# The order of six accumulating matmuls: by stationary tile, or by PSUM bank

## The chip, the cores and the metric

One Trainium2 chip; the kernel runs on one of its cores. The metric is the device time of the program in microseconds (us); smaller is better. The time before is 1608.74 us, the median of 3 runs.

## The reference

The program is one inference step of a small two-layer decoder, on 512 prompt tokens and 8 x 8 sample tokens, all in float32 (model width 1024):

```
x = x + rms_norm(mixer(rms_norm(x)))        # layer 0: chunked gated MLP, layer 1: RG-LRU block
x = x + rms_norm(swiglu(rms_norm(x)))
gmlp:   u, v = split(gelu(h @ w_in + b_in)); v = layer_norm(v); out = (u * (w_s @ v + b_s)) @ w_out
rglru:  y, xb = split(h @ w_in); conv of 4 taps; two gates by 8 blocks of 128x128; scan; out @ w_out
swiglu: g, u = split(h @ w_in); out = (silu(g) * u) @ w_out          # inner width 2816
```

Nearly all of the arithmetic is in the large products `h @ w`. Outputs are the two token results, the convolution and scan states, and the normalised `v` rows of the sample.

## The kernel before, in words

The 576 tokens lie on the free axis of all activations, which are stored transposed: feature tile by feature tile, 128 partitions x 576 columns. A product therefore has a 128x128 tile of the weights as its stationary operand and the activations as its moving operand. A PSUM bank takes 512 float32 columns, so an output tile of 576 tokens is a pair of banks, `2m` and `2m+1`, with 288 tokens (a "token half", `HT` = 288) in each. Four such pairs (`m` = 0 to 3) fill PSUM.

Every float32 product is done as three products of the reduced type `float32r`: the activation is split into a high part `hh` and a remainder `hl`, the weight into `whi` and `wlo`, and the result is `hh*whi + hl*whi + hh*wlo`. ScalarE makes the high parts (line 800 for weights), VectorE the remainders (line 1109). SyncE's queue loads weights into four slots of `stage` ahead of need.

A K step (`k`) of an output pair is thus six matmuls, three terms for each token half. The helper `three` (line 457) issues them. It is called by `u_body` (line 604), by the first and larger part of `out_phase` (line 644) and by `tile_unit` (line 722), in which one unit is one output pair over all 8 K steps. Its relative `one_half` (line 467) issues the three terms for one token half alone, all to one bank. It serves at the two kinds of stage border: in `first_tiles` (line 667), the first four output pairs of a projection, while the normalised activations are still arriving; and in the last four K steps of each group of `out_phase` (line 655), where half 0 is finished before half 1.

The order of the stages, with the start of the first matmul of 288 columns at 180 us: `V` (384-column matmuls with another helper, up to 180 us); `U`; then `out_phase("GO")`, `ffn_in("FI0")`, `out_phase("FO0")`, the `RI` projection with the recurrent block, `out_phase("RO")`, `ffn_in("FI1")`, `out_phase("FO1")`. Each `out_phase` has two groups (`G` = 0, 1) of four output pairs. In a group the K step is the outer loop and the pair `m` the inner one; in `tile_unit` the pair is fixed and K runs.

TensorE's instructions run in the order in which they are written. What other engines wait for are semaphores that the last matmul of a unit increments (`unit_done`, `y_tile_done`, `h_pair_used`); TensorE itself waits for weights (`lo_ready`), activations (`a_lo`, `h_lo`) and for a pair to be free (`pair_free[m]`, one semaphore for both banks of a pair). All of these waits stand ahead of a K step or a unit, none of them inside the six matmuls of `three`.

Of the kernel before, what the change touches and what calls it, by code (L numbers as in the profile page):

```python
# [38 lines left out]
def trunk_kernel(nc, x_prompt, x_sample, state_conv, state_h, norm_gains,  # L39
# [8 lines left out]
    HT = TT // 2  # L48
# [26 lines left out]
    with ExitStack() as ctx:  # L75
        def sb(name, shape, dt=F32):
            return ctx.enter_context(nc.sbuf_tensor(name, shape, dt))
# [6 lines left out]
        hh = sb("hh", [P, KD, TT], F32R)  # L84
        hl = sb("hl", [P, KD, TT], F32R)
# [53 lines left out]
        def half(h):  # L139
            return slice(h * HT, (h + 1) * HT)  # L140
# [63 lines left out]
        def xc(h):  # L204
            return wide[:, XC0 + h * TT:XC0 + (h + 1) * TT]
# [4 lines left out]
        def wg(mat, h):  # L210
            return wide[:, WG0 + (mat * KD + h) * P:WG0 + (mat * KD + h + 1) * P]
# [137 lines left out]
        def out_bank(b):  # L349
            return ps[0:P if PIECES[b][1] < NC else TS, OUT_BANK[b], :]  # L350
# [102 lines left out]
        def _(pe):  # L453
            def mm(out, w, x, start, stop):
                return pe.matmul(out, w, x, start=start, stop=stop)  # L455

            def three(m, hi_w, lo_w, k, first, last):

                a, b = ps[:, 2 * m, 0:HT], ps[:, 2 * m + 1, 0:HT]
                mm(a, hi_w, hh[:, k, 0:HT], first, False)  # L460
                mm(b, hi_w, hh[:, k, HT:TT], first, False)
                mm(a, hi_w, hl[:, k, 0:HT], False, False)
                mm(b, hi_w, hl[:, k, HT:TT], False, False)
                mm(a, lo_w, hh[:, k, 0:HT], False, last)
                return mm(b, lo_w, hh[:, k, HT:TT], False, last)

            def one_half(m, h, hi_w, lo_w, k, first, last):
# [39 lines left out]
            for k in range(KD):  # L507
                last = pe.transpose(ps[:, 7, k * TS:(k + 1) * TS], xin[NC][:, k * P:(k + 1) * P], ident[0:TS, 0:TS])
# [56 lines left out]
            for g in range(GRP):  # L565
                at = 4 * BANK + BANK + g * P if g < 4 else 6 * BANK + g * P - 4 * P
                last = pe.transpose(psf[:, at:at + P], wraw[:, g, :], ident[:, :])
# [7 lines left out]
            for k in range(KD):  # L575
                last = pe.transpose(ps[:, 5, 64 + 32 * k:96 + 32 * k], sraw[:, k * P:(k + 1) * P], ident[0:32, 0:32])
# [15 lines left out]
            def u_body(i, first=False, last_body=False):  # L592
                for c in range(6):
                    n = base["U"] + c
                    m = c % 3
                    pe.wait_ge(lo_ready, i * 6 + (n + 1))
                    if first and c < 3:
                        pe.wait_ge(z_evicted, NT * (GRP - 1) + min(2 * c + 2, NT))
                    else:
                        pe.wait_ge(pair_free[m], i * 2 + (c // 3))  # L600
                    for k in range(KD):
                        if last_body and c == 5 and k in (2, 5):
                            mix(i * 6 + 3 + k // 5, k // 5, 1, i * 2 + 1)
                        at = three(m, whi[:, slot(n), k * P:(k + 1) * P], wlo[:, slot(n), k * P:(k + 1) * P],
                                   k, k == 0, k == KD - 1)
                        if last_body and c == 5 and k % 2 and k < KD - 1:
                            at.then_inc(h_pair_used, 1)
                    at.then_inc(unit_done, 1)
                    if first and c < 2 or last_body and c == 5:
                        continue  # L610
                    if c % 3 == 2:

                        pe.wait_ge(ln_done, i * (2 * NT) + (c // 3 + 1) * NT)
                    gshift, f = divmod(c - 2, 3)
                    if first and c == 2:
                        pe.wait_ge(blk_landed, 16 * NB)
                        pe.wait_ge(rb_ready, 1)
                    mix(i * 6 + (c - 2), f, gshift % 2, i * 2 + gshift)
# [7 lines left out]
            def out_phase(name):  # L626
# [8 lines left out]
                for G in range(2):  # L635
                    first = base[name] + G * per
                    for j in range(per - 2):
                        pe.wait_ge(lo_ready, first + j + 1)
                        pe.wait_ge(a_lo, G * per + AB[name] + j + 1)
                        for kk in range(units[j][1]):  # L640
                            for m in range(4):
                                if j == 0 and kk == 0:
                                    pe.wait_ge(pair_free[m], G + free0[name][m])
                                last = three(m, *weights(first + j, kk, m), 2 * (j % 4) + kk, j == 0 and kk == 0, False)
                        last.then_inc(unit_done, 1)
# [72 lines left out]
            def tile_unit(n, m, freed, last_unit, i=0, per=0):  # L718
                pe.wait_ge(lo_ready, i * per + (n + 1))
                pe.wait_ge(pair_free[m], freed)  # L720
                for k in range(KD):
                    last = three(m, whi[:, slot(n), k * P:(k + 1) * P], wlo[:, slot(n), k * P:(k + 1) * P],
                                 k, k == 0, k == KD - 1)
                    if last_unit and k % 2 and k < KD - 1:
                        last.then_inc(h_pair_used, 1)
                last.then_inc(unit_done, 1)
# [21 lines left out]
            for mat in range(2):  # L748
                for h in range(KD):
# [3 lines left out]
                    for b in range(2):  # L753
                        last = mm(ps[:, 2 * (e % 4) + b, 0:HT], wg(mat, h), xc(h)[:, half(b)], True, True)
# [13 lines left out]
            for k in range(KD):  # L768
                last = pe.transpose(ps[0:36, 4 + k // 4, (k % 4) * P:(k % 4 + 1) * P], sout[:, k, :], ident[:, :])
            last.then_inc(so_turned, 1)  # L770
            pe.wait_ge(pair_free[3], free0["END"][3])
            for h in range(2):

                for k in range(KD):
# [7 lines left out]
                    for b, (hf, c) in enumerate(PIECES):  # L782
                        if hf == k // 4 and (c >= 2) == (h == 1):
                            r = P if c < NC else TS
                            last = pe.transpose(out_bank(b)[:, (k % 4) * P:(k % 4 + 1) * P],
                                                xT[:, k, c * P:c * P + r], ident[:, :])
# [916 lines left out]
```

## Time and profile before

| | |
|---|---|
| runs, us | 1607.57, 1608.74, 1609.88 |
| span of the profiled execution, first to last instruction, us | 1606.8 |
| TensorE busy (matmul) | 1564.4 us, 97%, 11250 instructions |
| TensorE busy (weight load) | 1538.5 us, 96%, 11250 instructions |
| VectorE busy | 796.9 us, 50% |
| ScalarE busy | 563.7 us, 35% |
| GpSimd busy | 302.7 us, 19% |
| HBM traffic | 82 GB/s over the span |

The profiled execution's own time is given as its span; no other time was recorded for it. Matmuls are pipelined: one of them lasts about 294 ns from its start to its end while the next starts 130 to 133 ns after it, so the durations of single matmuls overlap, and what counts in a dense stretch is the distance from start to start.

### The profile page before, as it was taken

What the parts mean: (1) busy time and instruction counts of PE and PEld (TensorE: products, weight loads), DVE (VectorE), ACT (ScalarE), POOL (GpSimd) and SP (SyncE); (2) the same over time, 40 slices, a digit from 0 to 9 for tenths busy, and PEclk for the clock granted to TensorE, in tenths of its full rate; (3) what the DMA queues carried; (4) which work ended last, traced back from release to release, by engine and by line L of the source; (5) the groups of instructions that cost most, each with busy time, mean ns of one, the idle gap of its engine ahead of it and who ended that gap; (6) DMA issues with size and microseconds to landing.
All of it is one profiled execution on the core that took longest, in us unless ns stands there. A gap on an engine that the chain in (4) does not pass through costs nothing.

```text
span 1606.8 us, 27610 instructions
## 1 busy us (share of the span) xinstructions
PE 1564.4 (97%) x11250; PEld 1538.5 (96%) x11250; DVE 796.9 (50%) x1033; ACT 563.7 (35%) x786; POOL 302.7 (19%) x260
## 2 busy tenths in 40 slices
PE   7999999999999899999999999997999999999997
PEld 7999999999999899999999989997899999999996
DVE  6444676674444832322353558767663233235444
ACT  5344422224343521212142434474442212124433
POOL 0100033331000412121110015336222121110002
PEclk9999999999999999999999999998999999999998
DMA  6322333322222133223232241122222232223211
GB/s 228 100 79 72 88 95 90 90 84 93 80 90 68 40 92 91 78 78 91 66 105 66 80 118 53 53 80 66 66 66 80 78 91 78 78 79 92 81 51 63
DMA packets 170498, 133.37 MB, mean 83 GB/s; under 512 B 4888, under 2 KB 147504, under 8 KB 170292
## 3 DMA queue, kind: packets, MB, share of 16 engines
q1 hardware_dynamic: 168756, 128.30, 26.6%
q0 software_dynamic: 1664, 3.95, 0.9%
q8 instruction: 58, 0.95, 0.2%
q14 instruction: 20, 0.16, 0.0%
HBM read 128.92 MB, written 3.29 MB: 82 GB/s over the span
## 4 chain that ended last, share of the span: by engine, by line
PE 88%; DVE 5%; POOL 2%; ACT 2%; issue 1%; DMA 0%; SPq 0%; ACTq 0%; POOLq 0%; DVEq 0%
PE ps L455 87%; DVE yb L1370 1%; DVE acc L1126 1%; DVE hl L1157 1%; POOL wide L1644 1%; DVE acc L1136 1%; ACT whi L800 0%; ACT wide L1070 0%; POOL sout L1643 0%; POOL s L1651 0%; DMA wide<-in_x_prompt_dram 0%; PE ps L517 0%; POOL sout L1642 0%; ACT wide L1076 0%; ACT yb L1071 0%
## 5 line engine op out<-in xcount | busy, mean ns | idle before, releaser
L455 PE MATMUL ps<-hh,whi 128*128 128x288 f32 x3264 | 745.3, 299 | 19.9 <-DVE hl L1157 6.7
L455 PE MATMUL ps<-hh,wlo 128*128 128x288 f32 x3264 | 736.8, 296 | 0.0
L455 PE MATMUL ps<-hl,whi 128*128 128x288 f32 x3264 | 736.0, 296 | 0.0
L455 PEld LDWEIGHTS ps<-hh,whi 128*128 128x128 f32 x3264 | 539.8, 189 | 28.5 <-issue 12.6
L455 PEld LDWEIGHTS ps<-hh,wlo 128*128 128x128 f32 x3264 | 540.7, 190 | 0.0
L455 PEld LDWEIGHTS ps<-hl,whi 128*128 128x128 f32 x3264 | 540.2, 190 | 0.5
L1109 DVE TENSOR_TENSOR wlo<-stage,whi 128x1024 fp32r<-128x1024 f32 (+2 forms) x240 | 284.3, 1188 | 317.0 <-ACT whi L800 316.7
L800 ACT ACTIVATE whi<-stage 128x1024 fp32r<-128x1024 f32 (+2 forms) x240 | 240.8, 1017 | 447.9 <-PE ps L455 430.7
L1613 POOL TENSOR_TENSOR wide<-wide,tmp 128x576 f32 x44 | 96.9, 2201 | 443.6 <-DVE tmp L1307 443.6
L1017 ACT ACTIVATE wide<-wide (+1 forms) x44 | 29.9, 685 | 332.5 <-DVE wide L1307 332.4
L1307 DVE TENSOR_TENSOR tmp<-ps,rb 128x576 f32<-128x576 f32 x76 | 57.4, 755 | 175.7 <-PE ps L455 175.7
L1167 DVE TENSOR_TENSOR hl<-wide,hh 128x1152 fp32r<-128x1152 f32 (+1 forms) x80 | 109.3, 1366 | 7.0 <-ACT hh L871 7.0
L1307 DVE TENSOR_TENSOR wide<-ps,rb 128x576 f32 (+1 forms) x44 | 33.1, 757 | 144.0 <-PE ps L455 136.9
L455 PE MATMUL ps<-wlo,hh 128*128 128x384 f32 (+1 forms) x320 | 99.9, 337 | 0.0
L871 ACT ACTIVATE hh<-wide 128x1152 fp32r<-128x1152 f32 (+1 forms) x80 | 88.5, 1107 | 29.5 <-POOL wide L1644 15.1
L1605 POOL TENSOR_TENSOR xT<-xT,yb 128x288 f32<-128x288 f32 x45 | 50.3, 1123 | 243.0 <-DVE yb L1370 243.0
L455 PE MATMUL ps<-whi,hh 128*128 128x384 f32 x264 | 90.4, 342 | 0.0
L455 PE MATMUL ps<-whi,hl 128*128 128x384 f32 x264 | 89.1, 338 | 0.0
L1581 POOL TENSOR_TENSOR wide<-wide,tmp 128x576 f32 (+1 forms) x24 | 53.0, 2210 | 111.3 <-DVE wide L1302 111.3
L455 PEld LDWEIGHTS ps<-wlo,hh 128*128 128x128 f32 (+1 forms) x320 | 56.3, 178 | 0.3
L1136 DVE TENSOR_TENSOR acc<-acc,tmp 128x288 f32<-128x288 f32 x56 | 30.9, 552 | 51.3 <-ACT tmp L846 51.1
L455 PEld LDWEIGHTS ps<-whi,hh 128*128 128x128 f32 x264 | 49.7, 188 | 0.7 <-issue 0.2
(153 smaller groups left out, 911.1 us busy)
## 6 DMA issues: line engine op xcount, KB each, us to landing
stage<-in_ffn_w_in_dram SPq DMA_DIRECT2D x88, 512.0 KB, 3.8
stage<-in_ffn_w_out_dram SPq DMA_DIRECT2D x40, 512.0 KB, 3.8
stage<-in_gm_w_in_dram SPq DMA_DIRECT2D x32, 384.0 KB, 3.6
stage<-in_gm_w_in_dram SPq DMA_DIRECT2D x24, 512.0 KB, 3.8
stage<-in_gm_w_out_dram SPq DMA_DIRECT2D x24, 512.0 KB, 3.8
stage<-in_rg_w_in_dram SPq DMA_DIRECT2D x16, 512.0 KB, 3.9
stage<-in_rg_w_out_dram SPq DMA_DIRECT2D x8, 512.0 KB, 3.7
wide<-in_x_prompt_dram SPq DMA_DIRECT2D x2, 1024.0 KB, 7.4
```

Of the source, the lines that this page charges most:

```text
L455: return pe.matmul(out, w, x, start=start, stop=stop)
L800: act.activation(whi[:, s, 0:width], stage[:, s, 0:width], ACT.Copy).then_inc(hi_ready, 1)
L871: act.activation(hh[:, at:at + nk, :].rearrange("p k n -> p (k n)"), source(name, k, nk), ACT.Copy).then_inc(a_hi, 1)
L1017: act.activation(w, w, ACT.Silu).then_inc(f_act, 1)
L1109: dve.tensor_tensor(wlo[:, s, 0:width], stage[:, s, 0:width], whi[:, s, 0:width].bitcast(F32), ALU.subtract).then_inc(lo_ready, 1)
L1126: dve.tensor_tensor(acc[:, at], acc[:, at], tmp[:, r % 3, at], ALU.add).then_inc(sq_added, 1)
L1136: dve.tensor_tensor(acc[:, half(h)], acc[:, half(h)], tmp[:, r % 3, half(h)], ALU.add).then_inc(psq_added, 1)
L1167: dve.tensor_tensor(hl[:, at:at + nk, :].rearrange("p k n -> p (k n)"), wide[:, src0:src0 + nk * TT], hh[:, at:at + nk, :].rearrange("p k ...
L1307: return dve.tensor_tensor(halves(out), pair(m), halves(rb[:, :]), ALU.mult)
L1581: pool.tensor_tensor(w, w, tmp[:, x % 3, :], ALU.mult).then_inc(gated, 1)
L1605: pool.tensor_tensor(x, x, yt(k)[:, half(h)], ALU.add).then_inc(res_ready, 1)
L1613: pool.tensor_tensor(w, w, tmp[:, c, :], ALU.mult).then_inc(ffn_gated, 1)
```

## The change

In `three`, the six matmuls of a K step are put in another order. Let a be the bank of token half 0 and b that of half 1. Before, the two halves alternate: a and b with `whi`,`hh`; a and b with `whi`,`hl`; a and b with `wlo`,`hh`. After, the three terms of a come first, then the three of b. In each bank the terms are added in the same order as before. The flags for the start and the end of the accumulation stay on the same matmuls, and the matmul that is returned, and on which a caller puts its semaphore increment, is the same one.

```diff
                 a, b = ps[:, 2 * m, 0:HT], ps[:, 2 * m + 1, 0:HT]
                 mm(a, hi_w, hh[:, k, 0:HT], first, False)
+                mm(a, hi_w, hl[:, k, 0:HT], False, False)
+                mm(a, lo_w, hh[:, k, 0:HT], False, last)
                 mm(b, hi_w, hh[:, k, HT:TT], first, False)
-                mm(a, hi_w, hl[:, k, 0:HT], False, False)
                 mm(b, hi_w, hl[:, k, HT:TT], False, False)
-                mm(a, lo_w, hh[:, k, 0:HT], False, last)
                 return mm(b, lo_w, hh[:, k, HT:TT], False, last)
```

## Rows read from the trace of the kernel before

**Rows 1.** The page: engines and their busy time, the chain that ended last.
```profile
PE 1564.4 (97%) x11250; PEld 1538.5 (96%) x11250; DVE 796.9 (50%) x1033; ACT 563.7 (35%) x786; POOL 302.7 (19%) x260
...
PE ps L455 87%; DVE yb L1370 1%; DVE acc L1126 1%; DVE hl L1157 1%; POOL wide L1644 1%; DVE acc L1136 1%; ACT whi L800 0%; ACT wide L1070 0%; POOL sout L1643 0%; POOL s L1651 0%; DMA wide<-in_x_prompt_dram 0%; PE ps L517 0%; POOL sout L1642 0%; ACT wide L1076 0%; ACT yb L1071 0%
```

**Rows 2.** Line 455: count, then ns shortest/median/longest, first and last start.
```profile
L455 PEld LDWEIGHTS ps<-hh,whi x3264: 186/188/337, 180.3 to 1586.0; 128*128 128x128 f32 x192
L455 PE MATMUL ps<-hh,whi x3264: 288/294/855, 180.4 to 1586.1; 128*128 128x288 f32 x192
L455 PEld LDWEIGHTS ps<-hl,whi x3264: 187/188/337, 180.6 to 1586.1; 128*128 128x128 f32 x192
L455 PE MATMUL ps<-hl,whi x3264: 289/294/442, 180.7 to 1586.3; 128*128 128x288 f32 x192
...
L455 PE MATMUL ps<-hh,wlo x3264: 288/294/442, 181.0 to 1586.4; 128*128 128x288 f32 x192
```

**Rows 3.** Windows of dense pair order, TensorE: us, busy (matmuls), clock, DMA.
```profile
561.50:872.50 311.00, 311.00 (x2335) 1.00 0.29 85
369.00:430.00 61.00, 61.00 (x460) 1.00 0.28 87
446.00:507.00 61.00, 61.00 (x472) 1.00 0.32 95
886.00:941.00 55.00, 55.00 (x425) 1.00 0.33 91
1518.20:1572.00 53.80, 53.80 (x416) 1.00 0.20 59
```

**Rows 4.** Timeline, one_half in half 0, FO0 group 0, 45 intervals: start, us.
```profile
873.10 0.30 PE L455 MATMUL ps<-hh,wlo 128*128 128x288 f32 x1
...
879.02 0.29 PE L455 MATMUL ps<-hh,wlo 128*128 128x288 f32 x1
```

**Rows 5.** Timeline, one_half in half 1, FO0 group 0, 33 intervals.
```profile
881.02 0.29 PE L455 MATMUL ps<-hh,wlo 128*128 128x288 f32 x1
...
885.42 0.30 PE L455 MATMUL ps<-hh,wlo 128*128 128x288 f32 x1
```

**Rows 6.** Timeline, change from half 0 to half 1, GO group 0.
```profile
438.58 0.29 PE L455 MATMUL ps<-hl,whi 128*128 128x288 f32 x1
438.71 0.29 PE L455 MATMUL ps<-hh,wlo 128*128 128x288 f32 x1
438.84 0.30 PE L455 MATMUL ps<-hh,whi 128*128 128x288 f32 x1
438.98 0.29 PE L455 MATMUL ps<-hl,whi 128*128 128x288 f32 x1
439.11 0.29 PE L455 MATMUL ps<-hh,wlo 128*128 128x288 f32 x1
439.25 0.30 PE L455 MATMUL ps<-hh,whi 128*128 128x288 f32 x1
```

**Rows 7.** Waits of TensorE, 560 to 1583 us: us in total, times, longest.
```profile
PE ps L455 <- DVE hl L1157: 4.5, 8, 1.0
```

**Rows 8.** Waits of VectorE, 561 to 872 us.
```profile
DVE wide L1307 <- PE ps L455: 68.8, 20, 4.6
DVE tmp L1307 <- PE ps L455: 67.4, 20, 4.4
DVE wlo L1109 <- ACT whi L800: 62.6, 28, 3.9
```

**Rows 9.** Timeline at the slow clock, one_half, RO group 0.
```profile
1116.03 0.44 PE L455 MATMUL ps<-hl,whi 128*128 128x288 f32 x1
1116.27 0.44 PE L455 MATMUL ps<-hh,wlo 128*128 128x288 f32 x1
```

## The prediction

> **What bounds the kernel now.** I read the page first. TensorE is busy for 97% of the span, no other engine for more than 50%, and 87% of the chain that ended last is line 455, the helper through which every large matmul goes [rows 1]. So the next view is that line by operands: three groups of 3264 matmuls of 288 columns, 9792 in all, each with a weight load of its own [rows 2]. The third is the list of waits. In the dense part from 560 to 1583 us the largest wait of TensorE sums to 4.5 us [rows 7], while VectorE, which empties PSUM, waits for TensorE for 68.8 and 67.4 us in one projection alone [rows 8]. No buffer, transfer or eviction decides there. What decides is the distance from the start of one matmul to the start of the next, and the change can act on nothing else. So the rest is about that distance.
>
> How to get it: a window's count holds, beside the matmuls that start in it, the two that were already running at its left edge (one lasts 294 ns). 311 us / (2335 - 2) = 133.3 ns; 61 us / (460 - 2) = 133.2 ns; but 61 us / (472 - 2) = 129.8 ns, 55 us / (425 - 2) = 130.0 ns and 53.8 us / (416 - 2) = 130.0 ns, all at full clock [rows 3]. The second and third of these windows are the same code in the same stage: group 0 and group 1 of GO, with the same weight slots, banks and activation addresses. **One instruction order runs at two rates**, 133.3 and 130.0 ns, and holds the one that it fell into at the start of the stretch. The distance is thus not a price per instruction but a rhythm which depends on how a stretch is entered. That is the main source of doubt below.
>
> **What the change moves.** Count of the matmuls that it touches: `one_half` issues 3 stages x 2 halves x 4 pairs x 8 K steps x 3 = 576 in `first_tiles` and 4 stages x 2 groups x 2 halves x 4 K steps x 4 pairs x 3 = 768 in the tails of `out_phase`. The other 9792 - 1344 = 8448 are from `three`, which is 1408 K steps. Group 1 of GO, FO0 and FO1 has 480, 432 and 432 of them: 1344 in the 130.0 ns rhythm [rows 3]. I take the other 7104 at 133.3 (the short RO stretches among them). Sum before: 7104 x 133.33 + 1344 x 130.0 = 947.2 + 174.7 = 1121.9 us, a mean of 132.8 ns.
>
> *Instructions added or removed*: none. Nor are semaphore increments: the last matmul of a K step stays the last. Bank a is complete three matmuls earlier, but nobody is told, so this brings nothing (3 x 0.13 = 0.4 us at most per pair, and evictions have slack, [rows 8]). No wait stands inside a K step, so none is moved. Cost 0.
>
> *Weight loads*: before, a stationary tile is used 4 times and then 2 times in a row; after, 2, 1, 2, 1. If a repeated load were cheaper than a new one, the change would lose it in two places per K step. The rows speak against it: the loads have the same count as the matmuls and medians of 188 ns whichever operand follows [rows 2], and `one_half`, which changes its tile twice in three matmuls, is no slower than `three` [rows 3 to 5]. Cost 0; the bounds are those of the distances below.
>
> The Trainium skill ("TensorE: Matmul & The Clock Gate", Part 2, step 1) says that a load and its matmuls are apart so that one can load once and then multiply repeatedly. By that rule the new order would need four loads where the old needed two. This trace disagrees with its premise here, 11250 loads standing beside 11250 matmuls. The same page (LDWEIGHTS) gives columns/1.2 ns, an estimate of 107 ns for 128; two more of them bare in 1408 K steps would be 300 us.
>
> *The distance in the new order.* The trace never shows a1 a2 a3 b1 b2 b3, but it shows its two halves. `one_half` in half 0 takes (879.02 - 873.10)/45 = 131.6 ns [rows 4]; in half 1 (885.42 - 881.02)/33 = 133.3 ns [rows 5]. So three matmuls in a row to one bank cost nothing by themselves; half 0 even runs below the usual pair rate. A new K step has 4 distances inside a half, 2 x 131.6 + 2 x 133.3 = 529.8 ns, and 2 distances between halves. For those two I have the pair order, all of whose distances are of that kind: 2 x 133.3 or 2 x 130.0. That gives 796.4/6 = 132.7 ns or 789.8/6 = 131.6 ns. With 8448 matmuls: 1121.3 or 1112.1 us, which is 0.6 or 9.8 us less than before. The bounds are wider. From below, the 130.0 rhythm everywhere: 1098.2 us, 23.7 less. From above, the one change of half that can be seen single, 438.98 to 439.11 to 439.25: the longest step there is 0.14 us [rows 6], and if both changes of half in a K step cost that, it is (529.8 + 280)/6 = 135.0 ns, 1140.2 us, 18.3 more. The rows at the slower clock show 240 ns [rows 9], which is 1.2 GHz against 2.4; that is the far end for a single matmul, but the granted clock follows from idle time and the change makes none.
>
> Which value do I take? The pair order holds a rhythm because its halves alternate one by one; in the new one the halves change every third matmul, so neither of the two pair rhythms can be kept as it is, and I expect the mean of the two sums: 132.2 ns, 1116.7 us, **5.2 us less than before**. The waits of the chain on other engines and the recurrent block do not change. The profiled span would be 1606.8 - 5.2 = 1601.6 us. The median of the runs is 1.9 us above that span, so the predicted time is 1608.7 - 5.2 = 1603.5 us, with 1599 to 1608.2 as this case's own range.
>
> **The rivals.**
>
> *Order is indifferent.* The distance is set by something that neither the bank nor the half touches, and the stretches stay near 133.3 ns. For: 133.3 is the commonest rate by far and is held by half 1 too [rows 3, 5]. Against: 130.0 and 131.6 exist. If all 8448 go at 133.3, the 130.0 stretches are lost: 1344 x 3.33 = 4.5 us more, 1613.2; if they survive, 1608.7.
>
> *The change of half costs (the other side).* Place: the first matmul of each half, 2816 times. Price: 0.14 us for the change, as at the one seen [rows 6], in place of 133.3 ns. With one in each K step: (529.8 + 133.3 + 140)/6 = 133.85 ns, 1130.8 us, 8.9 more, 1617.6 us; with both 1627. It decides as soon as the mean of the two changes is over (796.8 - 529.8)/2 = 133.5 ns. Against: the pair order makes such a change at every matmul and pays 133.3 at most on average.
>
> *The fast rhythm everywhere.* The new order falls into 130.0 ns in all stretches: 23.7 less, 1585 us. For: the rate exists for hundreds of matmuls. Against: no `one_half` stretch shows it, and only the strict alternation does.
>
> *Weight loads show.* The load of a new tile would not quite hide. `one_half` has two new tiles in three matmuls, `three` one in three; if the 1.6 ns between half 0 and the fast pair rhythm (131.6 against 130.0) were due to that, a new tile would cost 4.8 ns, and two more of them in 1408 K steps 13.5 us: 1622 us. Against: beside the common pair rate of 133.3 half 0 is faster with more new tiles [rows 3, 4].
>
> **How the numbers follow.** A change of 0.2%, 3.2 us, is about what a measurement of this kernel can tell from none. Chances: forecast 0.42, of which 0.30 beyond 3.2 us and 0.12 within; indifferent 0.24 (0.15 same, 0.09 slower, above 1612); change of half costs 0.16; fast rhythm 0.13; loads 0.05. Faster 0.30 + 0.13 = 0.43; same 0.12 + 0.15 = 0.27; slower 0.09 + 0.16 + 0.05 = 0.30. The range has to reach the fast rhythm on the one side and the first price of the change of half on the other: 1584 to 1619, leaving out perhaps 0.15.
>
> **What would show it.** Right: the window 561.5 to 872.5 us holds more than 2335 matmuls (2355 at 132.2 ns), half 0 and half 1 keep different rates, and groups 0 and 1 of GO come closer together. Wrong: 130.0 or 133.3 again in long stretches, by entry (a rhythm that knows no order); single steps of 0.14 us or more at each change of half; weight-load medians off 188 ns; or waits of VectorE for TensorE that change by more than the rate explains. The prediction fails most simply if the new order locks into a rhythm of its own that no stretch of this trace shows.

## The result: a little slower, and where

The changed kernel takes 1612.43 us (median of 6 runs, 1610.88 to 1614.96) against 1608.15 us (median of 6, 1605.52 to 1609.88). The ratio is 1.0029 with a 95% interval of 1.0016 to 1.0041: slower, by more than the measurement leaves open. The profiled spans are 1610.7 and 1606.8 us.

The same windows as in [rows 3], of the changed kernel (us, busy (matmuls), granted clock, DMA):

```profile
561.50:872.50 311.00, 311.00 (x2335) 1.00 0.29 84
369.00:430.00 61.00, 61.00 (x460) 1.00 0.27 87
446.00:507.00 61.00, 61.00 (x459) 1.00 0.29 87
886.00:941.00 55.00, 55.00 (x415) 1.00 0.25 78
1518.20:1572.00 53.80, 53.80 (x406) 1.00 0.19 59
```

The first window takes in FI0 and group 0 of FO0, the second is group 0 of GO. They did not move by one matmul: 2335 and 460, 133.3 and 133.2 ns from start to start. The other three, group 1 of GO, FO0 and FO1, had 472, 425 and 416 and now have 459, 415 and 406. Their distances are 61/457 = 133.5, 55/413 = 133.2 and 53.8/404 = 133.2 ns where they were 129.8 to 130.0. With 480 + 432 + 432 matmuls in these stretches, 1344 x 3.3 = 4.4 us is lost, about the difference of the medians (4.3) and of the profiled spans (3.9).

The rest that was looked at is as it was. The waits of TensorE from 560 to 1583 us and those of VectorE in FI0, to be held against [rows 7, 8]:

```profile
PE ps L455 <- DVE hl L1157: 4.5, 8, 1.0
```

```profile
DVE wide L1307 <- PE ps L455: 68.8, 20, 4.6
DVE tmp L1307 <- PE ps L455: 67.4, 20, 4.4
```

The weight loads keep their medians to within 1 ns (line 455; in [rows 2] they are 188 ns):

```profile
L455 PEld LDWEIGHTS ps<-hh,whi x3264: 186/187/337, 180.5 to 1589.8; 128*128 128x128 f32 x192
L455 PEld LDWEIGHTS ps<-hl,whi x3264: 187/188/337, 180.7 to 1590.0; 128*128 128x128 f32 x192
```

The timeline shows that a K step by bank is even. A half begins at each `ps<-hh,whi`; the steps to the ones at 700.41 and 700.81 are 0.13 us, and the two steps of 0.14 stand inside a half.

```profile
700.01 0.30 PE L455 MATMUL ps<-hh,whi 128*128 128x288 f32 x1
700.15 0.29 PE L455 MATMUL ps<-hl,whi 128*128 128x288 f32 x1
700.28 0.29 PE L455 MATMUL ps<-hh,wlo 128*128 128x288 f32 x1
700.41 0.29 PE L455 MATMUL ps<-hh,whi 128*128 128x288 f32 x1
700.55 0.29 PE L455 MATMUL ps<-hl,whi 128*128 128x288 f32 x1
700.68 0.29 PE L455 MATMUL ps<-hh,wlo 128*128 128x288 f32 x1
700.81 0.30 PE L455 MATMUL ps<-hh,whi 128*128 128x288 f32 x1
```

So the question was no longer what the new order costs, but what the 130.0 ns of three stretches had been, and whether the other 7104 matmuls could have it.

### The profile page after: what moved, and what is told of

It is laid out like the page before. It is cut to its first block, busy times and chain, and to the rows that moved or that the text cites. A ratio compares the mean times of both kernels' runs of the same rounds, so it can differ in the third digit from the quotient of the medians.

```text
span 1610.7 us, 27610 instructions
## 1 busy us (share of the span) xinstructions
PE 1569.9 (97%) x11250; PEld 1543.9 (96%) x11250; DVE 798.2 (50%) x1033; ACT 563.4 (35%) x786; POOL 302.5 (19%) x260
## 4 chain that ended last, share of the span: by engine, by line
PE 88%; DVE 5%; POOL 2%; ACT 2%; issue 1%; DMA 0%; SPq 0%; ACTq 0%; POOLq 0%; DVEq 0%
PE ps L455 87%; DVE yb L1370 1%; DVE acc L1126 1%; DVE hl L1157 1%; POOL wide L1644 1%; DVE acc L1136 1%; ACT whi L800 0%; ACT wide L1070 0%; POOL sout L1643 0%; POOL s L1651 0%; DMA wide<-in_x_prompt_dram 0%; PE ps L517 0%; POOL sout L1642 0%; ACT wide L1076 0%; ACT yb L1071 0%
## 5 line engine op out<-in xcount | busy, mean ns | idle before, releaser
L455 PE MATMUL ps<-hh,whi 128*128 128x288 f32 x3264 | 977.2, 299 | 19.5 <-DVE hl L1157 6.7
L455 PE MATMUL ps<-hl,whi 128*128 128x288 f32 x3264 | 965.1, 296 | 0.0
L455 PE MATMUL ps<-hh,wlo 128*128 128x288 f32 x3264 | 963.3, 295 | 0.0
L455 PEld LDWEIGHTS ps<-hh,whi 128*128 128x128 f32 x3264 | 615.3, 188 | 27.8 <-issue 12.6
L455 PEld LDWEIGHTS ps<-hh,wlo 128*128 128x128 f32 x3264 | 617.8, 189 | 0.0
L455 PEld LDWEIGHTS ps<-hl,whi 128*128 128x128 f32 x3264 | 615.9, 189 | 0.6
```

## The experiments

In all counts of windows below, 2 is taken off for the matmuls that were already running at the left edge. "Alternating" is the order of before. FI0 and FI1 are changed in the loops only (9 iterations of 4 units, a unit being one output pair with 48 matmuls), so one run carries several probes. Where a run gives the matmuls other columns, its numerical results are not the reference's; only its distances are used. Code cuts are shortened where they say so or show "...".

### Is it in the stretches at 130.0 alone?

Two complementary halves of the change. The first:

```diff
                 a, b = ps[:, 2 * m, 0:HT], ps[:, 2 * m + 1, 0:HT]
+                if in_group1[0]:          # second kernel: not in_group1[0]
+                    one_half(m, 0, hi_w, lo_w, k, first, last)
+                    return one_half(m, 1, hi_w, lo_w, k, first, last)
                 mm(a, hi_w, hh[:, k, 0:HT], first, False)
```

> Only the K steps of group 1 of the four out_phase stages go by bank (1440 matmuls); the other 7008 of three alternate as before. Theory R (the slowdown is the lost 130.0 ns rhythm of these stretches and nothing else): the whole loss is here, 1344 x 3.3 = 4.4 us, span 1611, although only a sixth of the matmuls is reordered. Theory G (the order by bank costs a little everywhere): a sixth of the loss, below 1 us.

Measured: 1612.62 us against 1608.27 (medians of 10 and 17 runs), ratio 1.0028 (1.0018 to 1.0037). A sixth of the reordered matmuls carries the whole loss. The three windows of group 1:

```profile
446.00:507.00 61.00, 61.00 (x460) 1.00 0.29 89
886.00:941.00 55.00, 55.00 (x415) 1.00 0.28 82
1518.20:1572.00 53.80, 53.80 (x406) 1.00 0.20 59
```

> The complement: everything by bank but group 1 of the out_phase stages, which alternates. Theory R: 7008 reordered matmuls cost nothing (133.3 or 133.0 ns either way), and group 1 may find its 130.0 ns again, since its entry (the tail in half 1) is the same: span 1606 to 1607. If instead the rhythm of group 1 is inherited from what group 0 had, it may be lost here: 133.3 ns in group 1 and span 1611. Theory G: 4 us slower whatever group 1 does.

Measured: 1612.59 us, ratio 1.0027 (1.0016 to 1.0038). Neither 1606 nor "the order costs a little everywhere": group 1 alternates here and is at 133.3 ns all the same in GO, FO0 and FO1 (x460, x414 and x406 in the same windows). Its rhythm is decided by what runs ahead of it, and the tail alone does not bring it to 130.0: behind a group 0 by bank, it did not. The effects of the two halves do not add up to the whole: each alone costs all of it.

### Parity, entry, or the form of the order?

The alternating order begun with the other half:

```diff
-                mm(a, hi_w, hh[:, k, 0:HT], first, False)
                 mm(b, hi_w, hh[:, k, HT:TT], first, False)
+                mm(a, hi_w, hh[:, k, 0:HT], first, False)
```

(and so for the other two couples.)

> The alternating order of before, but half 1 first and half 0 second in every K step. Two rates are known for the alternating order, 133.3 and 130.0 ns from start to start. Theory P (parity): a slow slot comes back every fourth matmul, and the rate depends only on which half stands in it, so to begin with the other half flips every stretch: FI0 (window 561.5 to 872.5 us) goes to 130.0 ns, about 2394 matmuls in the window, and group 1 of GO to 133.3; the span falls by about 7104 x 3.33 - 4.5 = 19 us, to 1588. Theory E (entry): the rate is decided by the state in which a stretch is entered, and the halves are alike: the long stretches stay at 133.3 ns and group 1 of GO, entered otherwise, may go either way; span 1602 to 1611. Theory O (the alternating order is fast only in this form): all at 133.3 or more, span 1611 or more.

Measured: span 1609.7 us, time 1610.99 (one run). FI0 holds 2335 matmuls and group 1 of GO 460: 133.3 ns everywhere. Theory P is out; O and E stand. (The tail ahead of group 1 still runs half 0 before half 1 here. Whether the mirrored order has a 130.0 rhythm behind the mirrored tail was not tested.) The next kernel puts extra matmuls ahead (two edits in one, shortened):

```diff
+                for _ in range(extra):        # FI0: 1 per iteration, FI1: 2; group 1: GO 1, FO0 2, RO 1, FO1 3
+                    mm(ps[:, 2 * m, 0:HT], whi[:, slot(n), 0:P], hh[:, 0, 0:HT], True, True)
```

> The kernel before with extra matmuls of 288 columns ahead of a stretch (their sums are overwritten, so that nothing changes in the result): one per loop iteration in FI0 and two in FI1, one at the start of group 1 of GO and RO, two in FO0, three in FO1. They cost 9 x 0.133 + 9 x 0.267 + 0.9 = 4.5 us. Theory P (the parity of the count of matmuls decides between 133.3 and 130.0 ns in the alternating order): in FI0 the iterations take turns at the two rates, FI1 stays as it is, group 1 of GO and FO1 goes to 133.3, that of FO0 stays at 130.0 and that of RO goes to 130.0. Theory E (each entry is decided by the timing of the few matmuls ahead of it): the groups 1 may go either way, and FI0 keeps 133.3 throughout.

Measured: span 1616.6 us. One, two or three extra matmuls at the entry, and group 1 is at 133.3 ns in all three stages; FI0 and FI1 stay at 133.3. A count modulo two doesn't decide. That leaves the entry, and it is easily spoiled. Windows of group 1 of GO, FO0, FO1:

```profile
449.00:509.00 60.00, 60.00 (x453) 1.00 0.31 93
892.00:944.00 52.00, 52.00 (x392) 1.00 0.30 87
1527.00:1581.00 54.00, 54.00 (x408) 1.00 0.19 59
```

### Bank, columns, or neither?

```diff
+                a, b = ps[:, 2 * m + swap, 0:n], ps[:, 2 * m + 1 - swap, 0:n]
+                xa, xb_ = slice(sa, sa + n), slice(sb_, sb_ + n)
-                mm(a, hi_w, hh[:, k, 0:HT], first, False)
-                mm(b, hi_w, hh[:, k, HT:TT], first, False)
+                mm(a, hi_w, hh[:, k, xa], first, False)
+                mm(b, hi_w, hh[:, k, xb_], first, False)
```

(and so for the other four matmuls; shown as if made to the kernel before.)

> The alternating order, in the loops of three stages with other operands; results are wrong in these. FI0: both halves read the columns of half 0 (the banks still alternate). FI1: both halves read the columns of half 1. U: the columns as before, but half 0 goes to the odd bank and half 1 to the even one. Theory A (address of the moving operand): columns of half 0 give the 131.7 ns that one_half shows in half 0, or less, in FI0; columns of half 1 give 133.3 ns in FI1; U does not change (133.3). Theory B (the bank decides): FI0 and FI1 are alike at 133.3, and U changes. Theory I (neither; an instruction stream of fixed pace): all three stay at 133.3.

Measured, windows in U (banks swapped), FI0 (columns of half 0), FI1 (columns of half 1):

```profile
200.00:360.00 160.00, 160.00 (x1185) 1.00 0.30 90
560.00:780.00 220.00, 220.00 (x1674) 1.00 0.29 85
1190.00:1410.00 220.00, 220.00 (x1652) 1.00 0.29 85
```

220/1672 = 131.6 ns with half 0's columns and 220/1650 = 133.3 with half 1's, though the banks alternate in both; swapping the banks in U left its dense stretches at 133.3 (39 distances of each unit are 133.0 or 133.4 ns on average, before and with the swap; the window above has the small mixing matmuls in it). Here the bank does nothing, though no run swaps it in a stretch at 130.0. What counts is from which columns the moving operand is read. The next two vary start and width.

> In the loops of FI0 and FI1 both halves read 288 columns from the same start column, another one for each of the four output pairs: 0, 32, 16, 64 in FI0 and 8, 48, 256, 288 in FI1; banks alternate as before and the results are wrong there. So far: from column 0 131.5 ns, from column 288 133.3. Theory A64 (what counts is the start within 64 columns, 256 bytes): 131.5 at 0, 64 and 256; 133.3 at 32 and 288, and at 8, 16, 48 too. Theory A32 (some other alignment, or the place in the tile): 64 or 256 unlike 0, or 32 unlike 288. Theory N (noise of the entry): the rates of the units do not go with the start column at all.

> As the run with start columns, but the start is column 0 for both halves and the width changes: 256, 264, 272, 280 in FI0; 240, 284, 286, 288 in FI1 (columns are left out, so results are wrong). What is over columns/2.4 was 11.5 ns at 288. Theory fixed: 11.5 ns at each width. Theory rounding (four matmuls together are rounded up to whole steps): the excess goes up and down between 10 and 13.3 with the width and the slope is not 1/2.4 from one width to the next. The weight load as a floor would show as a distance that no longer falls at 240.

Measured, mean distance of the last 36 matmuls of a unit, from the starts in the two traces (ns):

```
start column (288 wide)    0      16*          32      64      8       48      256     288
distance                   131.7  131.7         133.3   131.7   133.3   133.3   131.7   133.3
width (start 0)            240    256    264    272    280    284    286    288
distance                   112.0  120.0  120.0  125.2  127.8  131.1  128.9* 131.7
less width/2.4             12.0   13.3   10.0   11.8   11.1   12.8   9.7    11.7
* in half of the iterations; in the others 132.2 (start 16) and 133.3 (width 286)
```

The rows behind two start columns, 32 and 64, 36 distances each, and behind the width of 264, 42 distances:

```profile
594.04 0.43 PE L455 MATMUL ps<-hh,whi 128*128 128x288 f32 x2
...
598.84 0.43 PE L455 MATMUL ps<-hh,whi 128*128 128x288 f32 x2
...
606.76 0.42 PE L455 MATMUL ps<-hh,whi 128*128 128x288 f32 x2
...
611.50 0.42 PE L455 MATMUL ps<-hh,whi 128*128 128x288 f32 x2
```

```profile
638.23 0.41 PE L455 MATMUL ps<-hh,whi 128*128 128x264 f32 x2
...
643.27 0.40 PE L455 MATMUL ps<-hh,whi 128*128 128x264 f32 x2
```

With 288 columns, a start on a multiple of 64 columns (256 bytes) gives 131.7 ns; 8, 32, 48 and 288 give 133.3, and 16 takes turns at 131.7 and 132.2. In this run 264 columns take no longer than 256. The excess over the streamed columns moves between 9.7 and 14 ns and isn't a fixed cost, and a single width (286) can have two rates as well. Each start and each width stands behind one fixed neighbour, and two of them (16 and 286) change from one iteration to the next, so a part of these differences may be the entry and not the start or the width. That was not separated.

> The alternating order with fewer columns in each matmul in the loops of two stages; the results are wrong there, since columns are left out: 256 in FI0, 272 in FI1. At 2.4 GHz 288 columns are 120 ns, so 133.3 is 13.3 ns more and 130.0 is 10. Theory R (a remainder over a block of 128 columns makes the rhythm of four matmuls, 288 being 2 x 128 + 32): at 256 columns the rhythm is gone and the distance is 256/2.4 = 106.7 + 10 or less = 116.7 ns or less; at 272 (a remainder of 16, so a rhythm of eight) it is near 113.3 + 13 = 126. Theory F (fixed cost per matmul and weight load): 106.7 + 13.3 = 120.0 and 126.7 ns. Theory L (the weight load or the issue of instructions sets the pace): no shorter than 130 in both.

Measured: 190/1606 = 118.3 ns in FI0 and 200/1622 = 123.3 in FI1, an excess of 11.7 and 10.0 ns. Neither the fixed cost nor a floor by loads or issue, and the 118.3 is above what theory R allows. What sets the excess stays open. With two starts (0 and 288) these widths are also faster than with start 0 alone: 118.3 against 120.0 ns at 256 columns, 123.3 against 125.2 at 272. So that aligned starts are the fastest is shown for 288 columns only.

> The same 576 columns per K step, but cut as 320 + 256, so that both halves start at a multiple of 64 columns: alternating in the loop of FI0, by bank in that of FI1 (the evictions still take 288 of each bank, so results are wrong). In the loop of U: the order by bank with the columns of half 0 in both. If the start column makes the 133.3, the mean is 131.5 ns or less in all three, and the order by bank is then as fast as the alternating one: 311/131.5 + 2 = 2367 matmuls in 311 us in place of 2335. If the order by bank has a price of its own, FI1 and U stay at 133 ns while FI0 is faster.

Measured: FI0 and FI1 both at 200/1500 = 133.3 ns, with single distances from 117 to 150: the widths 256 and 320 bring their own excess, so my 131.5 was wrong for them. In U, order by bank and half 0's columns in both, a unit ran (308.70 - 303.56)/39 = 131.8 ns. That is what the alternating order had with half 0's columns in FI0 (131.6). So the order by bank has no price of its own; it has the pace of its columns.

> Alternating order in the loops of FI0 and FI1, but the two halves start at other columns, one couple for each of the four pairs (results wrong): (0,224) (16,240) (8,232) (24,248) in FI0, (32,256) (48,272) (56,280) (0,16) in FI1. Within 64 columns these are (0,32) (16,48) (8,40) (24,56) (32,0) (48,16) (56,24) (0,16). If a couple with one start on a multiple of 64 can hold either rhythm, (0,32) and (32,0) show 133.3 or 130.0 by unit; couples off the multiple on both sides are expected at 133.3, (0,16) between. A couple that is at 130.0 in all nine iterations would be a placement that makes the kernel faster by up to 23 us.

Measured (mean of the last 36 distances of a unit, ns, the same to 0.1 in all iterations but the first): (0,32) 133.1, (16,48) 132.2, (8,40) 133.3, (24,56) 133.4, (32,0) 133.1, (48,16) 132.2, (56,24) 133.2, (0,16) 133.3. None at 130.0 by its placement alone.

> Alternating order, but the 576 columns cut unevenly, the second half starting where the first ends, one cut for each of the four pairs (the evictions still take 288 of each bank, so results are wrong): 272+304, 280+296, 264+312, 256+320 in FI0, 284+292, 292+284, 304+272, 296+280 in FI1. 576 columns need at least 240 ns of streaming; 288+288 takes 266.7 or 260.0. If the excess comes by rounding as the widths and starts so far say, the sums lie between 260 and 273 and differ by cut: 256+320 at 266.7 as measured, and the cuts with an end near a multiple of 64 columns (264, 272) a little lower. If only the sum of the columns counts, all are at 266.7.

Measured (mean of both halves, ns): 272+304 131.7, 280+296 130.0, 264+312 130.0, 256+320 133.3, 284+292 131.7, 292+284 132.2, 304+272 132.6, 296+280 133.3. Two uneven cuts are at 130.0 in all nine iterations. This may be a second way to that rate; each cut was seen behind one neighbour only, and no whole kernel was built with one.

### Which entry leads to 130.0?

```diff
                     for c in range(4):
-                        tile_unit(base[name] + c, c, i + free0[name][c], False, i, 4)
+                        if c % 2: tile_unit(...)                  # alternating
+                        else: other_unit(..., kind, i, 4)         # FI0: by half, two steps; FI1: by bank, half 1 first
```

> In the loops of FI0 and FI1 every second unit has another order, and the unit behind it alternates as before, so each shows what rhythm an entry leaves: by half (24 and 24 matmuls) and by two K steps (6 and 6) in FI0; by bank (3 and 3) and by half with half 1 first in FI1. Results are the reference's. If an entry out of a long run of half 1 sets 130.0 ns, as at group 1 of GO, the unit behind by half is at 130.0 in every iteration and the one behind half 1 first is not. If it was chance, the units differ from iteration to iteration. If the alternating order falls back to 133.3 on its own, none is at 130.0.

Measured: behind a unit "by half" (24 matmuls of half 0, then 24 of half 1) the alternating unit ran at 130.0 ns in all nine iterations; behind the other three kinds never (133.3, 133.1 and 133.1 ns). The first such unit, its first and last couple, 46 distances, and the entry ahead of it:

```profile
564.55 0.29 PE L455 MATMUL ps<-hl,whi 128*128 128x288 f32 x1
564.69 0.30 PE L455 MATMUL ps<-hh,wlo 128*128 128x288 f32 x1
564.82 0.42 PE L455 MATMUL ps<-hh,whi 128*128 128x288 f32 x2
...
570.80 0.42 PE L455 MATMUL ps<-hh,wlo 128*128 128x288 f32 x2
```

This is what stands ahead of group 1 in `out_phase` as well: a tail with 48 matmuls of half 0 and then 48 of half 1.

> Every unit of an output pair in RI, FI0 and FI1 (but the last of each stage, and not U) does its 24 matmuls of half 0 and then its 24 of half 1, in place of the alternating order. If the two rates of one_half hold whatever stands around them (131.7 ns in half 0, 133.3 in half 1), the window 561.5 to 872.5 us holds 311/132.5 + 2 = 2349 matmuls and the span falls by about 4300 x 0.83 = 3.6 us to 1603. If the 131.7 comes only from the entry into those short stretches, it is 133.3 throughout: 2335 and no change. If a change of half costs, it is paid here once in 24 matmuls and not seen.

Measured: 190/1434 = 132.5 ns in FI0 and in FI1, as expected, time 1606.23 (one run). And something not expected: FI0's last unit, which alternates, and group 0 of FO0 behind it ran at 62/477 = 130.0, while group 1 of FO0 fell to 56/420 = 133.3, the reverse of before. Groups 0 and 1 of FO0, then of FO1:

```profile
807.00:869.00 62.00, 62.00 (x479) 1.00 0.32 97
883.00:939.00 56.00, 56.00 (x422) 1.00 0.32 92
1446.00:1501.00 55.00, 55.00 (x414) 1.00 0.30 96
1516.00:1570.00 54.00, 54.00 (x417) 1.00 0.18 59
```

That suggests a rule: **a run by half turns one rhythm of the alternating order into the other**. The others support it. In the kernel before and in ten of the others both groups of FO0 and FO1 have the order of before and the tail of before between them. In each of these, in both stages, one group is at 130.0 and the other at 133.3. The run with start columns has both cases, though the code of FO0 and FO1 is untouched: 54/416 = 129.8 and 55/413 = 133.2 ns in groups 0 and 1 of FO0, 133.2 and 130.1 in those of FO1. But the rule doesn't say in which rhythm a stage begins. In the run above, FI1 has the same code as FI0, and its last unit and group 0 of FO1 stayed at 55/412 = 133.5. The last kernels use the rule.

```diff
-                with pe.Fori(1, nb - 1) as i:
+                for c in range(4):
+                    tile_unit(base[name] + c, c, 1 + free0[name][c], False, 1, 4, by_half=c == 1)
+                with pe.Fori(2, nb - 1) as i:
```

with, in `tile_unit`, `for h in range(2): for k in range(KD): last = one_half(m, h, ...)` where `by_half` is set.

> The order of before, but one unit (the sixth) of FI0 and one of FI1 does its matmuls by half, 24 and 24; all others alternate. Theory E (a run of half 0 and then of half 1, entered without a stall from the 133.3 ns rhythm, leaves the alternating order at 130.0, and that holds until something disturbs it): the rest of FI0 and FI1, 34 units of 48 matmuls each, is at 130.0, the window 561.5 to 872.5 us holds about 2380 matmuls, and each stage gains 34 x 48 x 3.33 = 5.4 us, 10.9 in all. In group 0 of the out_phase behind it the 130.0 goes on (480 and 432 matmuls, 3.0 us more) and after its tail group 1 takes the other rhythm, as where group 0 was fast before (3.0 lost again): 1597 us. Theory C (a neighbour unit of another order is needed each time): only the next unit or two gain, 1608.

Measured: 1595.07 us against 1607.26, ratio 0.9925 (0.9912 to 0.9939). FI0 with most of group 0 of FO0, that group alone, group 1 of FO0, FI1 with most of group 0 of FO1:

```profile
572.00:862.00 290.00, 290.00 (x2233) 1.00 0.29 85
806.00:865.00 59.00, 59.00 (x456) 1.00 0.31 98
878.00:934.00 56.00, 56.00 (x422) 1.00 0.32 91
1198.00:1488.00 290.00, 290.00 (x2233) 1.00 0.29 85
```

290/2231 = 130.0 ns over a whole stage, held through all waits for weights and free pairs, and on into group 0 of FO0; then group 1 at 56/420 = 133.3. Two units of 48 matmuls in another order, where `three` has matmuls for 176, and 12 us.

> The changed kernel (three by bank) with the same two units by half. If the slow rate of the order by bank were only the fault of its entries, it would drop below 133 ns behind them, as the alternating order does. If the order itself cannot hold the fast rhythm, all stretches stay at 133.0 to 133.3 and the span is that of the changed kernel, 1611.

Measured: span 1613.6 us; the window 561.5 to 872.5 holds 2335 matmuls again, and group 1 of GO 460. With the entry that brings the alternating order to 130.0, the order by bank stays where it was. With its own columns (288 + 288) it shows no such rhythm in any stretch of any run here.

In the next one the first unit of group 1 in GO, FO0 and FO1 is done by half too:

```diff
+                        if G == 1 and j == 0 and name != "RO":
+                            for h in range(2):
+                                for kk in range(units[j][1]):
+                                    for m in range(4):
+                                        ...               # the wait for a free pair, as before
+                                        last = one_half(m, h, *weights(first + j, kk, m), ...)
```

> As the run before it, and the first unit of group 1 in GO, FO0 and FO1 does its matmuls by half too. If a run by half always turns one rhythm into the other, group 1 of FO0 and FO1 is turned back to 130.0 ns and that of GO, which is at 130.0 without it, falls to 133.3: against the run before it 2.8 us faster and 1.5 slower. If a run by half leads to 130.0 from either rhythm, all three groups are at 130.0 and it is 2.8 us faster. If it leads nowhere here because all four pairs take turns in it, no change or slower.

Measured: 1594.94 us, ratio 0.9918 (0.9905 to 0.9932); between it and the kernel before it the expected 1.3 us can't be told by time. The trace tells it, and the first branch came: a run by half turns either rhythm into the other. GO falls to 56/420 = 133.3, FO0 and FO1 come to 52/401 and 50/385 = 130 ns:

```profile
453.00:509.00 56.00, 56.00 (x422) 1.00 0.30 94
884.00:936.00 52.00, 52.00 (x403) 1.00 0.35 100
1509.00:1559.00 50.00, 50.00 (x387) 1.00 0.18 61
```

The rule in full: further units by half in group 0 of GO (the third unit) and in RI (the sixth and eleventh, `by_half=u == 5`, `by_half=u == 10`).

> As the last kernel with group 1, with further units by half where a stretch was left at 133.3 ns: the third unit of group 0 of GO, the sixth unit of RI and the eleventh (the first behind the gates). If a run by half turns one rhythm into the other wherever it stands, group 0 of GO goes to 130.0 behind it (about 380 matmuls), its tail turns that into 133.3, and the first unit of group 1 back to 130.0 (430 matmuls), and RI has about 300 matmuls more at 130.0: 1110 x 3.33 = 3.7 us below the run before, 1591 us. If the rhythm of RI does not follow, 1 us less of it. Against that theory would be any of these stretches at 133.3.

Measured: 1591.05 us against 1607.57 (1605.37 to 1610.12), ratio 0.9893 (0.9876 to 0.9909); the expectation was 1591. GO group 0 and group 1, FI0 (with group 0 of FO0), FO0 group 1, the two parts of RI, FI1 (with group 0 of FO1), FO1 group 1:

```profile
388.00:431.00 43.00, 43.00 (x333) 1.00 0.27 86
451.00:506.00 55.00, 55.00 (x425) 1.00 0.32 96
572.00:862.00 290.00, 290.00 (x2233) 1.00 0.29 85
882.00:934.00 52.00, 52.00 (x402) 1.00 0.35 101
999.00:1015.00 16.00, 16.00 (x126) 1.00 0.34 99
1047.00:1076.00 29.00, 29.00 (x225) 1.00 0.31 92
1200.00:1485.00 285.00, 285.00 (x2195) 1.00 0.29 86
1505.00:1555.00 50.00, 50.00 (x387) 1.00 0.18 58
```

All eight are at 130 ns. This kernel does the same multiplications and the same additions per bank as the one before, and is 1.1% faster than it and 1.4% faster than the changed one (0.9893/1.0029; the two were not timed side by side).

## Why the prediction was wrong, point by point

- **That only the distance from start to start decides**: right. The waits, the loads and the waits of VectorE stayed; the difference is the count of matmuls times 3.3 ns.
- **7104 matmuls at 133.3 and 1344 at 130.0**: right for the dense stretches, and the part of the working from which the true result (rival "order is indifferent", 1613.2 us with the fast stretches lost; measured 1612.43) follows. I gave that rival 0.24, and only 0.09 of it to a time above 1612. Some 30 matmuls in group 0 of RO ran at the slower level of the clock (240 ns, granted clock 0.50) and were counted at 133.3; they are the same in both kernels, so the difference doesn't change.
- **Weight loads, early end of bank a, waits: cost 0**: right, shown by medians and waits that did not move.
- **The step that failed** is the distance in the new order, "2 x 131.6 + 2 x 133.3" plus two of the pair order, and the mean of two sums, 132.2 ns. I priced it as if each distance belonged to its own half and could be added up. It is 133.3 for all six, the number that half 1 has alone. Half 0's 131.6 holds where every matmul reads from half 0's columns (U by bank, 131.8; FI0 alternating, 131.6) or from another start on a multiple of 64 (64, 256), and isn't carried into a K step that mixes the halves. That the mixture goes at 133.3 is measured; why it does isn't explained.
- **"Neither of the two pair rhythms can be kept"**: right for 130.0, and the very reason for the loss. I drew a mean from it instead of asking which of the two would be left.
- **The reading of the one change of half** [rows 6] took the wrong rows. Half 1 begins at 438.84, and the step to it is 0.13 us (438.71 to 438.84); the 0.14 that went into the upper bound and into the rival's price stand inside half 1.
- **The change of half costs**: not seen. **Fast rhythm everywhere**: not in this order, but a fact in another one. **Loads show**: no.
- **Sign and size**: forecast 5.2 us less, measured 4.3 us more; inside the range of 1584 to 1619, on the wrong side of no change.

The source of doubt that the prediction named, one order at two rates by entry, was the whole matter. I could have read more out of the trace of before: four `out_phase` stages, of which group 0 was never and group 1 three times at 130.0, with the same tail in between (RO, whose group 1 was not at 130.0, has waits in that tail).

## What to carry to other kernels

Where one engine is busy throughout, compare the distance from start to start, stretch by stretch, of code that is the same: two rates for one loop are a finding that no table of busy time shows, here worth 1.1%. A half of a change that alone costs as much as the whole suggests that the two halves act on one state, not on two costs. Before reordering an inner loop, ask which stretch runs faster than its twin and whether the new order can still do that.

## What the runs showed of the hardware

- The alternating order has two steady rhythms at full clock, 130.0 and 133.3 ns for 288 columns, and keeps either for more than 2200 matmuls, across semaphore waits that are already fulfilled. 24 or 48 matmuls of half 0 followed by as many of half 1 turn it from one to the other (seen both ways); 6 and 6, 3 and 3, and half 1 before half 0 did not bring it to 130.0, and one to three extra matmuls behind such a run spoil the turn. Nor did the turn come behind a stretch by bank (GO, FO0 and FO1) or into the mirrored order. RO is an exception: its group 1 was at 133.3 ns before and at 130.0 in four other kernels whose code is the same there (and in the one with only group 1 alternating). In the tail ahead of it TensorE waits twice (2.33 and 1.77 us before) and runs for some 3 us at the slower level of the clock (granted 0.50). The mechanism below this isn't settled.
- The PSUM bank had no part in the distances (banks swapped in U: 133.3 as before; with half 0's columns 131.6 ns in alternating banks and in one bank). The columns of the moving operand had: with 288 of them from one start, 0, 64 and 256 (multiples of 256 bytes) ran at 131.7 ns, the other starts at 131.7 to 133.3.
- Width isn't linear: from column 0, 264 columns cost what 256 do (120.0 ns). The Trainium skill ("TensorE: Matmul & The Clock Gate", Back-to-back issue gap) gives columns/2.4 plus 2.5 ns for what it calls the isolated gap between matmuls, an estimate of 122.5 ns for 288 columns, and says that in a stream with a weight load for each matmul the spacing is set by both. The matmuls here all have such a load, and no run came below 9.7 ns over columns/2.4; which part of that is the load was not measured.
